# Matrix products of a tile of ones in TensorE's three waits for the routing of a mixture of experts

## The chip, the cores and the metric

The kernel runs on one core of a Trainium2 chip. The metric is the device time of one execution in microseconds (us). TensorE (PE in the profile) has two clock levels in the rows, 1.2 and 2.4 GHz: the column PEclk gives the granted share, 0.50 for the lower and 1.00 for the upper.

## The reference, cut to what matters

One layer of an encoder on 512 tokens of width 1024: token mixing (retention and differential attention behind one input projection), then a mixture of 16 gated experts with two chosen for each token, then an embedding added under a gate. What surrounds the change is the choice of experts:

```python
lg = (t @ w_rg) + b_rg                      # 4 groups, the best one is taken
le = ((t @ w_re) + b_re).reshape(-1, 4, 4)  # 4 experts in each, the best two are taken
top_v, top_i = lax.top_k(le_sel, 2)
combine = one_hot(g_idx)[:, :, None] * w_in_group[:, None, :]
...
hid = silu(t @ w_gate[e]) * (t @ w_up[e]) * combine[:, e]
out = out + hid @ w_down[e]
```

All is float32. An expert has 4 MB of w_gate and w_up together and 2 MB of w_down; all 16 experts are loaded.

## The kernel before, in words

The kernel is written engine by engine, and the engines meet only through semaphores. Each engine works off its own list in the order in which it is written.

**Ahead of the routing.** TensorE makes the output projection with three products for each part (lines 1348 to 1350), transposes the new x (line 1519) and multiplies it by the router's weights (line 1532, 20 columns). VectorE adds the projection to x (line 1227, semaphore `x1_add`, which ends at 16) and norms it (line 1233). TensorE then transposes the input p of the last stage, eight transposes of 128x128 (line 1558).

**The routing**, on VectorE in `route()` (lines 971 to 1080), with TensorE used three times:

- VectorE finds the chosen experts and sums the membership (line 1014, `member_ready`). TensorE makes ranks from it in two products, line 1562 (ones times prefix, 80 columns) and line 1563 (64 columns), into `b_rank`.
- VectorE makes slots and one-hot tables from the ranks (lines 1022 to 1046, `slot_oh_ready`). TensorE sums with them the row numbers of every block, line 1567: two groups of eight products of 128x28, the first for the rows to be read, the second for the rows to be written.
- After the first group VectorE writes `src_row` (line 1054) and GpSimd issues the gathers of the first two blocks of rows (line 679). After the second it writes `dst_row` (line 1059) and the codes of the blocks (lines 1060 to 1070, `table_ready`).

**The experts.** The tokens are sorted by expert into blocks of 64 places, here 20 blocks. For a block TensorE transposes the gathered rows (line 1608, in `rows_transpose`), multiplies by w_gate and w_up (line 1622, in `gate_up`, 16 products of float32 that stand as 32 instructions), transposes the hidden part (line 1634) and multiplies by w_down (line 1648, in `down`). The order is: rows of block 0, `gate_up(0)`, rows of block 1, and then for each b: `hidden_transpose(b-1)`, `gate_up(b)`, rows of b+1, `down(b-1)`.

**The weights.** A ring of three places holds them. SyncE (SP, its queue SPq) issues the loads in a fixed order (line 586 for w_gate and w_up in halves, line 589 for w_down), and the load of expert e+3 waits until TensorE has used expert e: `gu_half_done`, `gu_done`, `dn_done`. The w_down of expert 2 waits for `table_ready` and for the gathered rows (lines 612 to 615). Experts 0 and 1 and the w_gate and w_up of expert 2 are under way before the routing ends.

**The clock.** At its start the kernel multiplies a tile of ones by itself 24 times before any data is there (line 1356), and 12 times while it waits for the first weights (line 1478). A float32 product stands as two matrix instructions and two weight loads in the trace.

Of the kernel before, what the change touches and what calls it, by code (L numbers as in the profile page):

```python
# [36 lines left out]
P = 128  # L37
SEQ, D = 512, 1024
NT = SEQ // P
# [31 lines left out]
OUT_UNITS = D // UC  # L71
# [136 lines left out]
def trunk(nc, x, p, norm_mix, w_in, lam_q1, lam_k1, lam_q2, lam_k2, diff_subln, w_out, norm_ffn,  # L208
# [3 lines left out]
    with ctx:  # L212
# [3 lines left out]
        def at(name, kb, shape, dt=F32):  # L216

            return nc.alloc_sbuf_tensor_at(name, shape, dt, offset=base + int(kb * K))
# [38 lines left out]
        ones = at("ones", 98.75, [P, P])  # L257
# [140 lines left out]
        b_proj = [bank[0], bank[1], bank[7]]  # L398
# [8 lines left out]
        def sem(name):  # L407
            return ctx.enter_context(nc.semaphore(name))
# [58 lines left out]
        x1_add = sem("x1_added")  # L467
# [874 lines left out]
        def _(pe):  # L1342
            T = nc.tensor
# [212 lines left out]
            for c in range(D_PLE // P):  # L1556
                for t in range(NT):
                    last = T.transpose(b_score[c][:, t * P:(t + 1) * P], p_sb[:, t, c * P:(c + 1) * P], ident)
                last.then_inc(p_T, 1)

            pe.wait_ge(member_ready, 1)
            T.matmul(b_rank[:, 0:80], ones[:], prefix[:].rearrange("p i e -> p (i e)"), start=True, stop=False)
            T.matmul(b_rank[:, 0:64], tri, member[:, 1:].rearrange("p i e -> p (i e)"), start=False, stop=True).then_inc(rank_done, 1)
            for w in range(2):
                pe.wait_ge(slot_oh_ready, 1 + w)
                for n in range(2 * NT):
                    last = T.matmul(b_rows[w],  # L1567
                                    slot_oh[:, n, :], blk_rows[:, w, n, :],
                                    start=(n == 0), stop=(n == 2 * NT - 1))
                last.then_inc(rows_done, 1)  # L1570

            pe.wait_ge(pT_ready, 2)
            pe.wait_ge(table_ready, 1)
# [166 lines left out]
```

## Time and profile before

| | |
|---|---|
| median of 3 runs | 637.39 us (636.6 to 638.26) |
| the profiled execution's own time | 636.99 us |
| its span, first to last instruction | 635.1 us |
| TensorE busy | 589.0 us, 93% of the span |
| mean granted TensorE clock | 0.967 |
| DMA packets | 151.52 MB, mean 239 GB/s |

Times in the rows count from the span's first instruction. The profiled execution's own time lies 1.9 us above its span. "issue" in the chain is time in which an engine waited for nothing that the profile shows. A number such as x32 behind a group counts instructions.

### The profile page before, as it was taken

The numbers are of one execution on the slowest core, as the hardware profiler recorded it, in microseconds if no ns is written. First come the engines' busy times: TensorE is split into PE (matmuls) and PEld (weight loads), VectorE is DVE, ScalarE is ACT, GpSimd is POOL, SyncE is SP. The second block draws the span as 40 slices with busy tenths as digits, with TensorE's granted clock in tenths as the row PEclk, the third lists the DMA queues.
The fourth block names the chain that finished last, engine by engine and source line by source line (L and its number), as shares of the span: only waits on it lengthen the run. The fifth ranks groups of instructions, "written<-read, shape, count | busy, mean of one in ns | idle before, by whom it ended". The sixth has DMA issues, their size and how long they took to land.

```text
span 635.1 us, 9546 instructions
## 1 busy us (share of the span) xinstructions
PE 589.0 (93%) x3496; PEld 386.2 (61%) x3497; DVE 209.7 (33%) x460; ACT 199.0 (31%) x435; POOL 51.1 (8%) x89
## 2 busy tenths in 40 slices
PE   9999999999999999975769999999999987998994
PEld 9988777878988999974223333333333332335883
DVE  4521365456344342265101111011011010164753
ACT  5622254545443543240100010010010010073774
POOL 0000000000000000001101211211212211110000
PEclk9999999999999999995789999999999999998998
DMA  9852214213220249737994799999999999934001
GB/s 310 221 203 99 71 63 133 67 32 101 68 67 1 67 160 419 316 136 296 362 418 183 296 418 425 422 418 422 419 422 422 420 421 421 393 120 179 34 33 66
DMA packets 47232, 151.52 MB, mean 239 GB/s; under 512 B 7896, under 2 KB 27232, under 8 KB 34656
## 3 DMA queue, kind: packets, MB, share of 16 engines
q1 hardware_dynamic: 43520, 139.77, 56.3%
q0 software_dynamic: 3392, 11.02, 4.4%
q8 instruction: 22, 0.36, 0.2%
q10 hardware_dynamic: 288, 0.29, 0.2%
q14 instruction: 10, 0.08, 0.0%
HBM read 141.62 MB, written 9.45 MB: 238 GB/s over the span
## 4 chain that ended last, share of the span: by engine, by line
PE 83%; DMA 5%; DVE 4%; issue 3%; SPq 2%; ACT 2%; DVEq 0%; POOL 0%; ACTq 0%; POOLq 0%
PE bank L1622 19%; PE bank L1348 13%; PE bank L1349 12%; PE bank L1350 12%; PE bank L1648 10%; DMA ring_dn<-in_w_down 5%; PE bank L1430 2%; PE bank L1681 2%; SPq L586 2%; PE bank L1608 2%; PE bank L1403 2%; PE bank L1356 1%; PE bank L1634 1%; PE bank L1567 1%; PE bank L1444 1%
## 5 line engine op out<-in xcount | busy, mean ns | idle before, releaser
L1622 PE MATMUL bank<-ring_gu,rowsT 128*64 128x512 f32 (+1 forms) x800 | 144.7, 602 | 6.4 <-DMA ring_gu<-in_w_up 2.8
L1622 PEld LDWEIGHTS bank<-ring_gu,rowsT 128*64 128x64 f32 (+1 forms) x800 | 43.9, 128 | 92.4 <-issue 88.1
L1648 PE MATMUL bank<-ring_dn,hidT 128*64 128x512 f32 (+1 forms) x400 | 74.7, 607 | 9.8 <-issue 5.2
L891 ACT ACTIVATE silu_g<-bank 128x256 f32<-128x256 f32 x20 | 7.7, 384 | 221.8 <-PE bank L1622 221.8
L1087 DVE TENSOR_TENSOR w_lo<-w_raw,w_hi 128x2048 fp32r<-128x2048 f32 x17 | 39.0, 2293 | 76.7 <-ACT w_hi L752 64.9
L1246 DVE TENSOR_TENSOR hid<-silu_g,bank 128x256 f32<-128x256 f32 x20 | 8.4, 421 | 147.9 <-ACT silu_g L891 147.9
L1348 PE MATMUL bank<-w_hi,hT_hi 128*128 128x256 f32 x192 | 55.5, 289 | 0.8 <-issue 0.6
L1349 PE MATMUL bank<-w_lo,hT_hi 128*128 128x256 f32 x192 | 54.3, 283 | 0.0
L1350 PE MATMUL bank<-w_hi,hT_lo 128*128 128x256 f32 x192 | 54.3, 283 | 0.0
L1348 PE MATMUL bank<-hT_hi,w_hi 128*128 128x512 f32 x128 | 50.9, 397 | 0.1
L1648 PEld LDWEIGHTS bank<-ring_dn,hidT 128*64 128x64 f32 (+1 forms) x400 | 21.0, 128 | 48.4 <-issue 42.3
L1349 PE MATMUL bank<-hT_lo,w_hi 128*128 128x512 f32 x128 | 50.0, 390 | 0.0
L1350 PE MATMUL bank<-hT_hi,w_lo 128*128 128x512 f32 x128 | 49.9, 390 | 0.0
L1260 DVE COPY y_blk<-bank 128x512 f32<-128x512 f32 x20 | 13.8, 692 | 80.7 <-PE bank L1648 80.7
L1348 PEld LDWEIGHTS bank<-w_hi,hT_hi 128*128 128x128 f32 x192 | 36.7, 191 | 2.6 <-issue 2.5
L1349 PEld LDWEIGHTS bank<-w_lo,hT_hi 128*128 128x128 f32 x192 | 36.8, 192 | 0.0
L1350 PEld LDWEIGHTS bank<-w_hi,hT_lo 128*128 128x128 f32 x192 | 36.8, 191 | 0.0
L752 ACT ACTIVATE w_hi<-w_raw 128x2048 fp32r<-128x2048 f32 x17 | 32.4, 1906 | 0.0
L1348 PEld LDWEIGHTS bank<-hT_hi,w_hi 128*128 128x128 f32 x128 | 24.0, 188 | 8.3 <-issue 3.6
L1348 PE MATMUL bank<-ple_hi,x2T_hi 128*128 128x512 f32 x64 | 25.8, 404 | 2.5 <-issue 2.5
L1350 PEld LDWEIGHTS bank<-hT_hi,w_lo 128*128 128x128 f32 x128 | 24.0, 188 | 5.1
L1349 PEld LDWEIGHTS bank<-hT_lo,w_hi 128*128 128x128 f32 x128 | 24.0, 188 | 4.7
(217 smaller groups left out, 892.7 us busy)
## 6 DMA issues: line engine op xcount, KB each, us to landing
ring_gu<-in_w_gate SPq DMA_DIRECT2D x32, 1024.0 KB, 12.3
ring_gu<-in_w_up SPq DMA_DIRECT2D x32, 1024.0 KB, 15.3
ring_dn<-in_w_down SPq DMA_DIRECT2D x16, 2048.0 KB, 21.5
w_raw<-in_w_in SPq DMA_DIRECT2D x13, 1024.0 KB, 5.0
w_raw<-in_w_out SPq DMA_DIRECT2D x4, 1024.0 KB, 4.9
ple_gate_raw<-in_w_ple_gate SPq DMA_DIRECT2D x1, 4096.0 KB, 28.9
yg<-y_rows SPq DMA_DIRECT2D x8, 512.0 KB, 7.2
xr<-in_x SPq DMA_DIRECT2D x4, 512.0 KB, 8.8
```

The source lines that it names most:

```text
L586: sp.dma_start(ring_gu[slot][:, n, ks, :], src[:, half]).then_inc(s_gu[slot][half], 16)
L752: nc.scalar.activation(w_hi[u % 2][:], w_raw[u % 2][:], ACT.Copy).then_inc(hi_done, 1)
L1087: V.tensor_tensor(w_lo[u % 2][:], w_raw[u % 2][:], w_hi[u % 2][:].bitcast(F32), ALU.subtract).then_inc(lo_done, 1)
L1260: V.tensor_copy(y_blk[buf][:], b_dn[:]).then_inc(y_ready, 1)
L1348: T.matmul(o, w_of(w[0], k), m_of(m[0], k), start=(k == 0), stop=False)
L1349: T.matmul(o, w_of(w[0], k), m_of(m[1], k), start=False, stop=False)
L1350: last = T.matmul(o, w_of(w[1], k), m_of(m[0], k), start=False, stop=(k == KD - 1))
L1403: last = T.matmul(b_score[2 * (i % 2) + c][:, 0:L], dqT[64 * c:64 * c + 64, h, i * P:(i + 1) * P], dkT[64 * c:64 * c + 64, h, 0:L], start= ...
L1430: last = T.matmul(b_o[:, i * P:(i + 1) * P], probsT[n % 2][:, o:o + P], v[:, j, h * P:(h + 1) * P], start=(j == 0), stop=(j == i))
L1608: last = T.transpose(b_xT[:, j * P:(j + 1) * P], rows[buf][:, j::4], ident)
L1622: last = T.matmul(b_gu[q * BLK + t:q * BLK + t + n, :], rowsT[:, k % 4, k // 4, t:t + n], ring_gu[s][:, :, k, q * UC:(q + 1) * UC], start= ...
L1648: last = T.matmul(b_dn[q * BLK + t:q * BLK + t + n, :], hidT[:, kf % 2, kf // 2, t:t + n], ring_dn[s][:, kf, q * (D // 2):(q + 1) * (D // 2)],
```

## The change

TensorE gets a helper that multiplies the 128x128 tile of ones by itself n times into the first 128 columns of the bank `b_proj[2]`, whose last sum has been taken when `x1_add` is 16. It is called with 10, 14 and 10: before the wait for `member_ready`, after the rank products, and after the row-number products. Nothing is removed, and no other engine's list changes.

```diff
                 last.then_inc(p_T, 1)
 
+            def kept_warm(n):
+                for _ in range(n):
+                    T.matmul(b_proj[2][:, 0:P], ones[:], ones[:], start=True, stop=True)
+
+            pe.wait_ge(x1_add, NT * OUT_UNITS)
+            kept_warm(10)
             pe.wait_ge(member_ready, 1)
             T.matmul(b_rank[:, 0:80], ones[:], prefix[:].rearrange("p i e -> p (i e)"), start=True, stop=False)
             T.matmul(b_rank[:, 0:64], tri, member[:, 1:].rearrange("p i e -> p (i e)"), start=False, stop=True).then_inc(rank_done, 1)
+            kept_warm(14)
             for w in range(2):
                 pe.wait_ge(slot_oh_ready, 1 + w)
                 for n in range(2 * NT):
...
                 last.then_inc(rows_done, 1)
+
+            kept_warm(10)
 
             pe.wait_ge(pT_ready, 2)
             pe.wait_ge(table_ready, 1)
```

## Rows read from the trace of the kernel before

**Rows 1.** The page's clock line, in 40 equal slices of the span.
```profile
PEclk9999999999999999995789999999999999998998
```

**Rows 2.** Stretches: busy us of each engine, PEclk, DMA share, GB/s.
```profile
core 0: us, PE busy (x) PEld busy (x) DVE busy (x) ACT busy (x) POOL busy (x), PEclk, DMA share, GB/s
340.00:350.00 10.00, 10.00 (x52) 3.56 (x52) 1.45 (x3) 0.98 (x2) 1.05 (x2) 1.00 0.43 171
360.00:545.00 185.00, 178.46 (x1016) 61.47 (x1014) 22.68 (x47) 14.71 (x30) 35.80 (x61) 1.00 1.01 421
```

**Rows 3.** TensorE's timeline near the end of the experts: start, us, group, idle before.
```profile
539.62 3.65 PE L1648 MATMUL bank<-ring_dn,hidT 128*64 128x512 f32 x16 [1.84 <-DMA ring_dn<-in_w_down]
```

**Rows 4.** SyncE's timeline: two weight loads that follow one another.
```profile
336.05 0.38 SPq L589 DMA_DIRECT2D ring_dn<-in_w_down  x1
353.02 0.34 SPq L586 DMA_DIRECT2D ring_gu<-in_w_gate  x1
```

**Rows 5.** The chain that ended last, from the ranks to the first product with w_down: start, us.
```profile
286.82 0.72 PE bank L1562 x2
287.54 0.41 PE bank L1563 x2
...
291.82 7.04 PE bank L1567 x32
...
301.75 0.99 issue
302.74 1.14 PE bank L1608 x4
...
304.73 9.75 PE bank L1622 x32
...
317.55 7.09 PE bank L1622 x32
324.64 0.68 PE bank L1608 x4
325.32 5.16 issue
330.47 5.38 PE bank L1648 x16
```

**Rows 6.** Short stretches around changes of clock or pace, columns as in rows 2.
```profile
5.50:6.00 0.50, 0.50 (x4) 0.50 (x4) 0.00 (x0) 0.47 (x3) 0.00 (x0) 1.00 1.03 285
6.50:7.00 0.50, 0.50 (x7) 0.50 (x6) 0.00 (x0) 0.00 (x0) 0.00 (x0) 1.00 1.07 360
...
282.50:282.75 0.25, 0.25 (x3) 0.06 (x1) 0.22 (x2) 0.25 (x1) 0.00 (x0) 1.00 0.00 0
282.75:283.00 0.25, 0.04 (x1) 0.00 (x0) 0.21 (x2) 0.25 (x2) 0.00 (x0) 0.57 0.62 246
...
310.00:310.25 0.25, 0.25 (x4) 0.14 (x2) 0.00 (x0) 0.00 (x0) 0.00 (x0) 0.82 0.89 328
```

**Rows 7.** Ones (chain), and the work ahead of the first wait (timeline).
```profile
0.98 8.15 PE bank L1356 x48
10.01 2.68 PE bank L1478 x24
...
280.81 0.97 PEld L1532 LDWEIGHTS bank<-w_r,x1T 128*128 128x128 f32 x8 [1.13 <-ACT x1T L851]
281.72 1.07 PE L1558 MATMUL bank<-small,p_sb 128*128 128x128 f32 x8
```

**Rows 8.** The first gather (timeline), gathers' time to landing, a stretch.
```profile
296.67 1.03 POOL L679 DMA_INDIRECT rows<-h_rows,src_row  x1 [294.69 <-DVE src_row L1054]
...
rows<-h_rows,src_now POOLq DMA_INDIRECT x20, 7.1
rows<-h_rows,src_row POOLq DMA_INDIRECT x2, 3.5
...
296.00:298.00 2.00, 2.00 (x11) 2.00 (x11) 0.62 (x1) 0.00 (x0) 1.03 (x2) 0.50 0.08 33
```

## The prediction

> **What bounds the kernel now.** I read the stretches first, then the chain, then the clock. From 360 to 545 us the DMA engines are full (share 1.01, 421 GB/s) and the clock is 1.00; near its end TensorE waits for w_down [rows 2, 3]. So the experts' second half is bound by bytes. But from 340 to 350 us the DMA share is 0.43 with TensorE busy all the time [rows 2]: SyncE has issued a load at 336.05 and issues the next at 353.02, when TensorE is halfway through `gate_up(3)` [rows 4]. The stream of weights that fills the rest of the kernel starts when TensorE lets it. What TensorE gains before 353 us brings the stream forward, and with it the end; what it gains between 353 us and the last weights is hidden behind them.
>
> The chain of that stretch is TensorE and VectorE in turn [rows 5]: ranks at 286.82, row numbers from 291.82 to 298.86, table ready at 301.75, transposes at 302.74, `gate_up(0)` for 9.75 us, `gate_up(1)` for 7.09 us. The two products are the same work, so 2.66 us of the first are the clock. It is the only low place of length in the clock line, slices 19 to 21, about 286 to 333 us [rows 1]. In short stretches one sees the edges: 1.00 until 282.75, then 0.57 in the quarter in which the last transpose ends, and up again in the quarter from 310.00 [rows 6]. Thus the ranks, the row numbers, the rows' transposes and over half of `gate_up(0)` run at 1.2 GHz.
>
> **The price of the ones.** 24 of their matrix instructions at the upper level take 2.68 us, 0.112 us each; the 48 at the start take 8.15 us [rows 7]. With twice 0.112 us at the lower level, n of 48 low gives 0.223n + 0.112(48-n) = 8.15, so n = 25 or 5.6 us. The stretches show the pace change from 4 to 7 starts in half a microsecond in that place [rows 6] (the PEclk column reads 1.00 there from the start; the pace is the witness). So a run of these products alone did raise the clock here, after 5 to 6 us.
>
> **Part 1, ten products before the ranks** (20 instructions: 2.2 us at 2.4 GHz, 4.5 us at 1.2). They start behind the transposes at 282.8; the ranks' wait ends at 286.82, 4.0 us of cover. The clock falls at 282.8, before the first of them has run, so they can't prevent that fall; I take them as starting low. Low throughout they end at 287.3 and cost 0.5 us; if the clock comes back on the way they cost nothing. I take a cost of 0.2, ends 0 and 0.5.
>
> **Part 2, the ranks.** 0.72 + 0.41 = 1.13 us at 1.2 GHz [rows 5]; at 2.4 at best half, a gain of 0 to 0.5. I take 0.4. VectorE's work behind them, 287.95 to 291.82 (3.87 us), moves with them.
>
> **Part 3, fourteen products after the ranks** (28 instructions: 3.1 us high, 6.2 low). The cover is those 3.87 us. High they cost nothing; low they make the row numbers 2.4 us late. I take 0.
>
> **Part 4, the row numbers.** 32 instructions in 7.04 us, 0.22 each, at 1.2 GHz. The nearest rows at 2.4 GHz are the router's loads of 128 columns before 20 moving columns: eight from 280.81 until the next line's work at about 281.7, 0.11 each [rows 7]. So at best the 7.04 us become 3.5. I don't take all of it: in the trace 7 us of these narrow products left the clock low, and it fell after about two microseconds of 20-column products and transposes. I expect the first group high and the second low or the reverse: a gain of 1.75, ends 0 and 3.5.
>
> A rule speaks against this part. The Trainium skill (TensorE: Matmul & The Clock Gate, section "LDWEIGHTS") gives a weight load as its columns over 1.2, with no regard to the clock. By it the row numbers, which are loads above all, would gain nothing, and the sum below would be 1.75 less. The rows disagree, 0.22 us each low against 0.11 high, and I go by the rows.
>
> **Part 5, ten products after the row numbers.** The cover is the way to the transposes, 298.86 to 302.74, 3.9 us: 2.2 us high are hidden, 4.5 low are 0.6 late. I take 0. If this work were not there, nothing else would hold the clock in that wait.
>
> **Beside it: the gathers.** The first is issued at 296.67, just as the weights' transfer has drained (share 0.08 in 296 to 298), and lands in 3.5 us; with full queues a gather takes 7.1 [rows 8]. With the first group ready some 2.2 us sooner it is issued at 294.5 into a full queue and lands between 298.0 and 301.6. The table asks for the transposes at 302.74 - 1.95 = 300.8, so it costs 0 to 0.8 us; I take 0. SyncE's load of w_down behind it isn't used before block 2.
>
> **Part 6, transposes and `gate_up(0)`.** 1.14 against 0.68 us is a gain of 0.46, and 9.75 against 7.09 one of 2.66 [rows 5], if the clock is up at their start.
>
> **Sum.** -0.2 + 0.4 + 1.75 + 0.46 + 2.66 = 5.1 us sooner at the end of `gate_up(0)`. What follows up to 353 us is on the chain and moves with it: the gap of 5.16 us before the first `down` too, behind which that product takes 5.38 us instead of 3.65 [rows 3, 5]. Whether the clock falls in that gap again I can't tell; I assume that it does, and 1.7 us more are to be had if not. The loads of 301 to 333 us are not in the way, since the DMA share of 0.43 leaves room to come forward by more than this. Against the profiled time, 636.99 - 5.1 = 631.9; the median of the runs stands 0.4 above it, so I predict **632.3 us**.
>
> **Rivals.**
>
> *The clock is lost again before `gate_up(0)`* (0.12). The last things before it are transposes and a wait. For it: it fell at 282.8 right behind the p transposes. Then only 0.4 - 0.2 + 1.75 = 1.95 us are gained, 635.4, and `gate_up(0)` still takes 9.75. The Trainium skill (same page, "PE-mode transpose") says that a transpose doesn't count as work for the clock; the fall at 282.8 behind eight of them agrees.
>
> *Slower: the ones run low throughout* (0.06). If neither the first ten nor the fourteen raise the clock, the ranks start 0.5 late, the fourteen take 6.2 us against a cover of 3.87 and make the row numbers 2.4 later, and the last ten another 0.6: 3.5 us, 640.9. The point is whether the clock is up before about 289, while the fourteen run. Against it: alone at the start the ones did raise it.
>
> *Hidden after all* (0.05). If the weights' stream rather than TensorE sets the start of the bound part, 637.4. For it: the share of 1.01; against it: 0.43 in 340 to 350.
>
> *The loads of weights don't follow the clock* (0.04). 5.1 - 1.75 = 3.3 us, 634.1. This is the page's rule of part 4.
>
> *The change does nothing* (0.03). The products run in the waits, but the clock stays as it was where it matters, and no wait is lengthened: 637.4.
>
> *The forecast* has 0.70, from 3.5 to 7.1 us (part 1 at 0, part 2 at 0.5, part 4 at 3.5) with up to 1.7 for `down(0)`.
>
> **Numbers.** Low end: 637.4 - 7.1 - 0.7 (part of the 1.7) = 629.6. High end: up to the case in which the clock is lost, 635.4 and half a microsecond of scatter, 635.9. A measurement of this kernel can tell about 0.3%, 1.9 us, so faster is below 635.5: the forecast 0.70, the rule's rival 0.04 and half of the lost clock 0.06, together 0.80. Same: the other half 0.06, 0.05 and 0.03, together 0.14. Slower 0.06.
>
> **What would show it.** Part 1: 20 instructions of ones from 282.8, PEclk 0.50 at first, 1.00 before 288. Part 4: the row numbers in 3.5 to 5.5 us instead of 7.04. Part 6: `gate_up(0)` near 7.1 us, its start near 300 to 302. The load of 353.02 issued about 5 us sooner, the same share of 1.01 from there on. I am wrong if the clock reads 0.50 when `gate_up(0)` starts, if the row numbers wait for ones, or if the load at 353 comes sooner and the end doesn't.

## The result, and the profile after

The changed kernel takes 629.38 us (median of 4 runs, 626.58 to 631.16) against 637.83 us before in the same comparison: 8.4 us less, ratio 0.9852 with an interval of 0.9824 to 0.988. The forecast was 632.3 us in a range from 629.6; the direction was right, the gain forecast too small, and the median lies 0.2 us under the range. The profiled execution of the changed kernel took 630.97 us, 1.6 above its median.

The page's head, its clock line and its row for the queue that carries instructions:

```profile
span 629.1 us, 9682 instructions
...
PEclk9999999999999999998899999999999999988998
...
q8 instruction: 23, 0.38, 0.3%
```

The 136 instructions more are the 34 products of ones, two matrix instructions and two weight loads each. The clock line has two places of 8 where [rows 1] have 5, 7, 8. One more low place has come up late, at slice 36.

The chain that ended last, in the same stretch as [rows 5] (start, us, what; L1563 is now the ones, L1568 and L1569 the ranks, L1574 the row numbers, L1617 the rows' transposes, L1631 `gate_up`, L1643 the hidden transposes, L1657 `down`):

```profile
286.52 0.45 PE bank L1568 x2
...
287.18 4.81 PE bank L1563 x28
291.98 1.72 PE bank L1574 x16
...
294.92 3.54 DMA rows<-h_rows,src_row
298.46 0.90 issue
299.36 0.76 PE bank L1617 x4
...
300.97 8.80 PE bank L1631 x32
...
312.71 7.09 PE bank L1631 x32
...
320.48 0.72 issue
321.20 3.65 PE bank L1657 x16
324.86 0.91 issue
...
326.27 1.46 issue
327.72 8.78 PE bank L1631 x32
```

Against [rows 5]: the transposes come at 299.36 instead of 302.74, and `gate_up(0)` takes 8.80 instead of 9.75 us. The product of `gate_up(0)` ends at 309.77 instead of 314.48, 4.7 us earlier. Then comes what the forecast had not: the gap of 5.16 us before the first `down` is 0.72 us, and there is one of 0.91 behind it. With the gap gone `down(0)` takes 3.65 instead of 5.38 us, but `gate_up(2)` falls into a low clock and takes 8.78 us instead of 7.09, so that these two cancel. By 336.5, the end of `gate_up(2)`, TensorE is 8.0 us ahead.

Two stretches show where the clock is low now (columns as in [rows 2]), and SyncE's load that answers to the second of [rows 4]:

```profile
287.50:291.00 3.50, 3.50 (x19) 3.50 (x18) 3.26 (x11) 0.00 (x0) 0.00 (x0) 0.51 1.01 426
301.00:305.00 4.00, 4.00 (x12) 1.31 (x14) 0.00 (x0) 1.24 (x2) 0.97 (x1) 0.57 0.93 336
```
```profile
344.99 0.34 SPq L586 DMA_DIRECT2D ring_gu<-in_w_gate  x1
```

The load is issued 8.03 us earlier. From there the DMA engines are full, and what TensorE has gained arrives at the end, less 2 us: the last `down` fell into a low clock in this execution (5.35 us where it took 3.65 before), which is the late place in the clock line.

```profile
549.88 5.35 PE L1657 MATMUL bank<-ring_dn,hidT 128*64 128x512 f32 x16 [0.84 <-DVE hidT L1251]
```

So the 8 us at 345 us have two parts: about 4.7 up to the end of `gate_up(0)` (0.3 of them because VectorE is 0.3 earlier from long before the change), and 3.3 behind it. The second part stands where neither a product of ones nor a change of clock was expected. Two theories can explain it. **Code**: 34 products more move all of TensorE's later instructions, code comes in transfers of 16 KB, and a transfer that TensorE had to wait for while the DMA engines were full is no longer in that place. **Clock**: all of it follows from the clock, through the times at which transfers start.

### The profile page after: what moved, and what is told of

It reads as the page before. It is cut to its first block, busy times and chain, and to the rows that moved or that the text cites. A ratio compares the mean times of both kernels' runs of the same rounds, so it can differ in the third digit from the quotient of the medians.

```text
span 629.1 us, 9682 instructions
## 1 busy us (share of the span) xinstructions
PE 595.5 (95%) x3564; PEld 391.3 (62%) x3565; DVE 209.7 (33%) x460; ACT 199.3 (32%) x435; POOL 51.3 (8%) x89
## 4 chain that ended last, share of the span: by engine, by line
PE 82%; DMA 7%; DVE 3%; issue 3%; ACT 2%; SPq 2%; DVEq 0%; POOLq 0%; ACTq 0%
PE bank L1631 19%; PE bank L1348 13%; PE bank L1349 13%; PE bank L1350 13%; PE bank L1657 10%; DMA ring_dn<-in_w_down 5%; PE bank L1430 2%; PE bank L1690 2%; SPq L586 2%; PE bank L1617 2%; PE bank L1403 2%; PE bank L1643 1%; PE bank L1444 1%; DMA gmix<-in_norm_mix 1%; PE bank L1563 1%
## 5 line engine op out<-in xcount | busy, mean ns | idle before, releaser
L1631 PE MATMUL bank<-ring_gu,rowsT 128*64 128x512 f32 (+1 forms) x800 | 145.5, 604 | 5.1 <-issue 2.9
L1631 PEld LDWEIGHTS bank<-ring_gu,rowsT 128*64 128x64 f32 (+1 forms) x800 | 44.1, 128 | 91.4 <-issue 87.8
L1657 PE MATMUL bank<-ring_dn,hidT 128*64 128x512 f32 (+1 forms) x400 | 76.4, 616 | 5.5 <-DMA ring_dn<-in_w_down 4.0
L1657 PEld LDWEIGHTS bank<-ring_dn,hidT 128*64 128x64 f32 (+1 forms) x400 | 21.5, 129 | 45.4 <-issue 39.1
```

The costliest lines, as they stand in the source:

```text
L1631: last = T.matmul(b_gu[q * BLK + t:q * BLK + t + n, :], rowsT[:, k % 4, k // 4, t:t + n], ring_gu[s][:, :, k, q * UC:(q + 1) * UC], start= ...
L1657: last = T.matmul(b_dn[q * BLK + t:q * BLK + t + n, :], hidT[:, kf % 2, kf // 2, t:t + n], ring_dn[s][:, kf, q * (D // 2):(q + 1) * (D // 2)],
```

## The experiments

**The same code without the work.** The tile of ones is replaced by products of one column by one column in the same places:

```diff
+            def tiny(n):
+                for _ in range(n):
+                    T.matmul(b_proj[2][0:1, 0:1], ones[:, 0:1], ones[:, 0:1], start=True, stop=True)
...
-            kept_warm(10)
+            tiny(10)
...
-            kept_warm(14)
+            tiny(14)
...
-            kept_warm(10)
+            tiny(10)
```

> All 34 products of ones become products of one column by one column in the same places: the same number of TensorE instructions and the same code size as in the changed kernel, and next to no matrix work. Code theory (part of the gain is that TensorE's code lies elsewhere, so that the 5.16 us gap before the first down product is gone whatever the clock does): the gap is about 0.7 us as in the changed kernel, the clock is low from 283 to about 310 as before, gate_up(0) takes near 9.7 us, and the time is 2 to 4 us under the kernel before, 634 to 636. Clock theory (all comes from the clock): the gap stays at 5 us and the time is that of the kernel before, 637 to 638.

Measured: 633.77 us (5 runs), before 638.2 (14 runs), ratio 0.9945, 0.9926 to 0.9963. Code alone, with hardly any work, makes the kernel faster: 4.4 us by the medians, 3.5 by the ratio. Its chain:

```profile
301.76 0.99 issue
302.76 1.14 PE bank L1621 x4
...
304.75 9.62 PE bank L1635 x32
...
325.84 1.03 issue
326.88 5.34 PE bank L1661 x16
```

Up to `gate_up(0)` it is the kernel before, to within 0.15 us: the clock is low for it. The gap ahead of `down` (L1661) is 1.03 us, with one of 0.70 ahead of the transposes. The clock theory expected 637 to 638 and a gap of 5 us; it falls as the only cause.

**The work with the old place of the code.** Thirty one-column products are added to the changed kernel, 256 TensorE instructions in all, matrix products and weight loads together. If an instruction takes 64 bytes, they are the 16 KB of one transfer:

```diff
             kept_warm(10)
+            tiny(15)
...
             kept_warm(10)
+            tiny(15)
```

> The changed kernel with 30 one-column products more (15 behind the first ten products of ones, 15 behind the last ten), so that 256 matrix instructions are added in all where the change adds 136. One transfer of code carries 16 KB; if an instruction takes 64 bytes, all code behind lies at the same place within its 16 KB as in the kernel before. Code theory: the gap of about 5 us before the first down product comes back, and the time is 2 to 4 us above the changed kernel, 631 to 634. Clock theory: the time of the changed kernel, 628 to 630, with at most 0.5 us for the longer waits.

Measured: 636.23 us (10 runs), ratio 0.9968, 0.9945 to 0.9992. The gap is back, 5.82 us, although the row numbers take 3.9 us, nearly all at the upper clock:

```profile
291.76 3.90 PE bank L1579 x32
...
321.80 5.82 issue
327.62 6.20 PE bank L1663 x16
```

It took 2 us more than expected. The gap lets the clock fall again: `down` takes 6.20 us instead of 3.65. And the third wait was overfilled: ones and one-column products end at 300.28, so that the transposes come at 300.68, 1.3 us later than in the changed kernel. Whether the two explain all of the 2 us isn't shown.

**The fourth corner**: 64 one-column products and no ones, 256 instructions too.

```diff
-            kept_warm(10)
+            tiny(20)
...
-            kept_warm(14)
+            tiny(24)
...
-            kept_warm(10)
+            tiny(20)
```

> The kernel before with 64 one-column products in the three waits (20, 24, 20) and no product of ones: 256 matrix instructions added and nearly no matrix work. Code theory: with 16 KB of code added, the code behind lies in its transfers of 16 KB as in the kernel before; the gap of about 5 us before the first down product is back and the time is that of the kernel before, 637 to 638.5. Rival, any addition of code takes the gap away or the one-column products help by themselves: 633 to 635, as with 34 of them.

Measured: 637.28 us (10 runs), before 638.51 (19 runs), ratio 0.9981, 0.9963 to 0.9999. The gap is there, and the time is that of the kernel before but for at most a few tenths of a per cent:

```profile
324.92 5.64 issue
330.56 6.43 PE bank L1661 x16
```

The four corners don't simply add up. Without the gap the ones take the time from 633.8 to 629.4 us; with it only from 637.3 to 636.2, and there the intervals of the two ratios overlap.

**Other amounts of code.** Eight and twenty one-column products behind the first ten of ones, and 42 of them without ones:

```diff
             kept_warm(10)
+            tiny(8)
```


> The changed kernel with 8 one-column products behind the first ten of ones: 32 instructions or 2 KB more code, otherwise the same. Code theory: the gaps ahead of the first gate_up, down and hidden transposes move by 2 KB of code; if none comes to lie on the wrong side of a transfer, 628 to 631 as the changed kernel, else up to 5 us more. Clock theory: 628 to 631.

```diff
             kept_warm(10)
+            tiny(20)
```


> The changed kernel with 20 one-column products behind the first ten of ones: 80 instructions or 5 KB more code, between the changed kernel (no large gap) and the one with 120 instructions more (a gap of 5.8 us). Code theory: the sum of the gaps before block 3 lies between theirs and names where the large gap begins; 629 to 636. Clock theory: 628 to 631.

```diff
-            kept_warm(10)
+            tiny(18)
...
-            kept_warm(14)
+            tiny(14)
...
-            kept_warm(10)
+            tiny(10)
```


> The kernel before with 42 one-column products (18, 14, 10) and no product of ones: 168 instructions, the code size of the changed kernel with 8 one-column products. Code theory: the large gap before the first down product is away as with 34 of them, 632 to 635. Rival, that the 34 one-column products won by chance of the clock: 637 to 638.

Measured: 627.15 us (4 runs), 635.83 (10 runs) and 634.25 (4 runs, ratio 0.9929, 0.9906 to 0.9953). The first two differ by twelve cheap products, 48 instructions, and by 8.7 us; the third, 168 instructions without ones, stays near the 633.8 us of 136. With twenty the gap has come back in another place, between `down(0)` and the hidden transposes (L1648), and the low clock behind it is in `gate_up(2)`:

```profile
321.33 4.08 PE bank L1662 x16
325.41 6.01 issue
331.42 0.69 PE bank L1648 x2
332.11 1.25 issue
333.37 9.93 PE bank L1636 x32
```

One count sorts all of them. The queue q8 carries instructions; in the stretch from 300 to 350 us, the first pass through the experts' code, it has this row in the changed kernel and the next in the kernel before:

```profile
q8 instruction: 4, 0.07, 0.5%
```
```profile
q8 instruction: 5, 0.08, 0.6%
```

| kernel | instructions added | ones | transfers of q8, 300 to 350 | longest gap, us | load that starts the bound part, us | median, us |
|---|---|---|---|---|---|---|
| before | 0 | no | 5 | 5.16 | 353.02 | 637.8 to 638.5 |
| 34 one-column | 136 | no | 4 | 1.45 | 348.78 | 633.8 |
| 42 one-column | 168 | no | 4 | 1.59 | 349.03 | 634.3 |
| 64 one-column | 256 | no | 5 | 5.64 | 353.01 | 637.3 |
| changed | 136 | 34 | 4 | 1.46 | 344.99 | 629.4 |
| changed, 8 more | 168 | 34 | 4 | 1.66 | 344.76 | 627.2 |
| changed, 20 more | 216 | 34 | 5 | 6.01 | 351.78 | 635.8 |
| changed, 30 more | 256 | 34 | 5 | 5.82 | 350.05 | 636.2 |

Four transfers and no long gap, or five and one of 5 to 6 us, whatever the ones do. The other profiles of this document with the weights' loads left as they were have four, and no gap above 1.6 us. A transfer less in this stretch isn't a transfer less in all: the changed kernel and those with 136 or 168 one-column instructions have one at 295 to 297 us, during the routing, where the kernel before has none. How a 16 KB block comes to be late for just one place, and why 216 instructions move the gap behind `down(0)`, isn't shown.

**Is the gap a transfer under load?** The kernel before, with SyncE held back until the first `down` is done:

```diff
+            sp.wait_ge(dn_done, 1)
             reload_gu(RING, 0)
```

> The kernel before with one wait more on SyncE: the loads of expert 3 and later are not issued before the first down product is done, so that the DMA engines are empty when TensorE comes to the 5.16 us gap. If the gap is a transfer of TensorE's code that is slow because it shares the DMA engines with 4 MB of weights, it shrinks to 1 to 3 us here; if it is a cost of TensorE's own, it stays at 5. The time isn't the question: the weights come later, and I expect 637 to 650.

Measured in one execution each: 640.22 us beside 638.16. The weights come later, as expected. With TensorE's code as before and five transfers in the same stretch, the gap is gone and `down` follows the transposes at once. Its chain, and then a stretch ahead of the gap in this kernel and in the kernel before (DMA share 0.12 against 1.02):

```profile
324.44 0.68 PE bank L1609 x4
325.12 3.58 PE bank L1649 x16
```
```profile
318.00:324.00 6.00, 6.00 (x30) 1.93 (x26) 0.00 (x0) 0.00 (x0) 0.00 (x0) 1.00 0.12 40
```
```profile
318.00:324.00 6.00, 6.00 (x30) 2.08 (x28) 0.00 (x0) 0.00 (x0) 0.00 (x0) 1.00 1.02 422
```

The row of q8 for 318 to 333 us, first in the kernel before, then in this one:

```profile
q8 instruction: 3, 0.05, 1.3%
```
```profile
q8 instruction: 4, 0.07, 1.6%
```

By the trace the three start at 320.55, 326.50 and 332.40 us, 5.9 us apart, and TensorE stands still from 325.32 to 330.47. The four start at 318.08, 321.13, 324.20 and 327.26, 3.1 us apart. A transfer's own packet lasts about 1 us in both; what grows under load is the distance from one to the next.

So the 5 us need both: a transfer of code in that place, and DMA engines full of weights.

**Which ones do what.** With the code size of the changed kernel, only the last ten are of ones, or only the first 24:

```diff
-            kept_warm(10)
+            tiny(10)
...
-            kept_warm(14)
+            tiny(14)
...
             kept_warm(10)
```


> Only the last ten products are of ones, the first 24 are of one column: the code size of the changed kernel. If the clock for the row numbers is what the first 24 bring, the row numbers take 7.0 us here instead of 3.5 and the time is about 3 us above the changed kernel, 632 to 633, with the clock up in part of gate_up(0) because of the last ten. If the last ten products alone bring nothing for gate_up(0), it takes 9.7 us and the time is that of the kernel with one-column products everywhere.

```diff
             kept_warm(10)
...
             kept_warm(14)
...
-            kept_warm(10)
+            tiny(10)
```


> The first 24 products are of ones, the last ten of one column: the code size of the changed kernel. If the last ten hold the clock for gate_up(0), it takes about 9.7 us here instead of 8.8 or 7.1, and the time is 1 to 2.5 us above the changed kernel, 630 to 632. If the clock holds without them, the time is that of the changed kernel, 628 to 630. The row numbers take 3.5 us in either case.

Measured: 630.36 us (ratio 0.9895, 0.987 to 0.9921) and 630.39 us (0.9887, 0.987 to 0.9904), 4 runs each: 1 us above the changed kernel and 3.4 us under the one with none. TensorE's timelines, first with the last ten only, then with the first 24 only:

```profile
291.85 7.03 PE L1578 MATMUL bank<-blk_rows,slot_oh 128*128 128x28 f32 x32 [3.11 <-DVE slot_oh L1045]
298.70 3.98 PE L1563 MATMUL bank<-ones 128*128 128x128 f32 x20
...
304.39 7.09 PE L1635 MATMUL bank<-ring_gu,rowsT 128*64 128x512 f32 x32 [0.87 <-ACT rowsT L886]
```
```profile
291.41 3.75 PE L1578 MATMUL bank<-blk_rows,slot_oh 128*128 128x28 f32 x32 [0.70 <-DVE slot_oh L1045]
295.10 0.64 PE L1567 MATMUL bank<-ones 128*1 128x1 f32 x20
299.07 1.12 PE L1621 MATMUL bank<-small,rows 128*128 128x128 f32 x4 [3.33 <-DMA rows<-h_rows,src_row]
301.06 9.72 PE L1635 MATMUL bank<-ring_gu,rowsT 128*64 128x512 f32 x32 [0.87 <-ACT rowsT L886]
```

In the place behind each filling it divides cleanly. The first 24 buy the row numbers, 7.03 to 3.75 us; the last ten buy `gate_up(0)`, 9.72 to 7.09. In time it doesn't: either half alone is worth 3.4 us, both together 4.4. With the last ten only, `gate_up(1)` falls into the low clock instead and takes 8.78 us, and the time is 1.6 us below the 632 to 633 that were expected.

**Closing the last gaps.** In the changed kernel's profile the clock is low from 301 us, at the start of `gate_up(0)`, behind the wait for the gathered rows and the one for their evacuation. Both are filled:

```diff
-            kept_warm(10)
+            kept_warm(16)
...
             rows_transpose(0, 1)
+            kept_warm(3)
```

> The changed kernel with 16 instead of 10 products of ones in the third wait and 3 more between the first transposes of rows and gate_up(0), where TensorE waits 0.87 us. If the clock fell at the start of gate_up(0) because of the two waits ahead of it, it now stays up: gate_up(0) in 7.1 us instead of 8.8, and the time is 1 to 2 us under the changed kernel, 627 to 629. If the fall comes all the same, the time is that of the changed kernel or 0.5 us over it. The code grows by 36 instructions, 2.3 KB, as in the kernel with 8 one-column products.

Measured: 627.08 us (4 runs), ratio 0.9815, 0.9778 to 0.9852. It was timed again beside the changed kernel:

> The kernel with 16 products of ones in the third wait and 3 more ahead of gate_up(0), once more. If the clock at the start of gate_up(0) is what it gains over the changed kernel, it is 1 to 2 us under it here too, 626 to 629; if its 2.3 KB of code more were the cause instead, it should equal the kernel with 8 one-column products, 627, and both its gaps and the clock in the profile tell which.

> The changed kernel once more, timed beside the next one on the same chip. Both theories: 628 to 631.

Measured: 626.21 us (5 runs, ratio 0.9821, 0.98 to 0.9841) against 629.31 us for the changed kernel (6 runs, 0.9869, 0.9847 to 0.9892) on the same chip. It is the fastest version here, 12.1 us or 1.8% under the kernel before. In both profiles `gate_up(0)` takes 7.11 us; the first of them:

```profile
302.51 7.11 PE bank L1635 x32
```

This was the expectation, but it doesn't account for the gain. In the profile of the changed kernel that was taken beside it, `gate_up(0)` takes 7.11 us too, without the added ones. Pieces of the two chains, first the changed kernel's, then that of the one with both waits filled:

```profile
300.42 7.11 PE bank L1631 x32
...
318.16 0.71 issue
...
322.53 1.51 issue
...
324.54 1.36 issue
325.90 8.78 PE bank L1631 x32
```
```profile
311.86 8.78 PE bank L1635 x32
...
325.34 0.47 issue
```

Each has one `gate_up` at the low clock, `gate_up(2)` in the first and `gate_up(1)` in the second. What differs are the waits around `down(0)` that stand as "issue", 3.6 us against 0.5, which leave the second 1.8 us ahead when the load that starts the bound part is issued (343.17 and 341.38). Nearly all the rest between these two executions is the last `down`, 5.35 against 3.65 us. So the 3.1 us between the medians are shown as a gain, but not as one of the clock at `gate_up(0)`, and how much of them the 2.3 KB of code more make isn't settled: the changed kernel with 2 KB more code and no more ones reached 627.15 us, though with only 4 runs spread over 4.4 us.

## Why the prediction was wrong

**The step that failed** is in the sentence behind the sum: "What follows up to 353 us is on the chain and moves with it: the gap of 5.16 us before the first `down` too". I had the gap in front of me as "issue", an engine that waits for nothing that the profile shows, and took an unexplained wait for a constant. By the experiments it was a wait for TensorE's own code, and 34 products are 136 instructions of code. In the changed kernel the waits from the transposes of block 1 to `gate_up(2)`, 5.16 and 1.16 us before, are 0.72, 0.91 and 1.46. The rule was at hand. The Trainium skill (Advanced Engine Details and Errata, section "ISA Cache") says that instructions are cached in lines of 16 KB, each of 256 instructions. The runs agree: a transfer of q8 carries 16 KB, 256 instructions added bring the gap back, and 136 and 168 take it away; 216 bring one back too, in another place. The forecast held no price for code at all, for or against; the same change with 80 instructions more takes 635.8 us, 2.7 us under the kernel before.

What the code was worth with no ones: 638.2 to 633.8 us. What the ones were worth at equal code: 633.8 to 629.4 us, 4.4 us, where the sum had 5.1. The missing term is thus about as large as the one I had. They aren't independent: the forecast kept the gap, and with the gap in place (30 one-column products more) the ones reached only 636.2 us, 2.0 under the kernel before, part of the shortfall being the overfilled third wait. That the forecast of 632.3 us came within 3 us of the result is in part luck.

The sentence behind that step, on `down(0)`, was wrong too. I assumed that the clock falls in the gap again, and put 0.7 of the 1.7 us into the low end of the range. With the gap gone the product took 3.65 us, the whole 1.7; `gate_up(2)`, which the forecast didn't price, lost as much.

**Part 1** said that the clock falls at 282.8, before the first product of ones. In the changed kernel's profile it didn't: the first ten took 2.40 us at the upper level, and the fall came at 287.5, among the fourteen. In its second profile the ten took 3.52 us, partly low, and in the kernel with the first 24 only 3.87 us. Both occur, so the place of the fall isn't tied to the transposes' end as one trace had made it look. The ranks were on time in all three.

**Part 2**, 0.4 forecast: 1.13 to 0.66 us, 0.5. Right.

**Part 3**, no cost forecast: the fourteen took 4.81 us, part of them low, against a cover of 3.87, and the row numbers began 0.9 us late. For this execution the choice of 0 was wrong by 0.9. In the second profile the fourteen ran at the upper level, 3.34 us, and cost nothing, so the term varies from run to run.

**Part 4**, 1.75 forecast, ends 0 and 3.5: 7.04 to 3.5 us, the whole of it. Clock and loads go together: 32 pairs of load and product take 7.03 us at 0.50 and 3.65 to 3.75 at 1.00 in the timelines. The Trainium skill's figure for a weight load, the same at either clock (TensorE: Matmul & The Clock Gate, section "LDWEIGHTS"), doesn't fit these rows; the measurement decides, and that rival is out.

**Part 5 and the gathers**, no cost: table and gathered rows were ready within 0.1 us of each other. The first gather landed in 3.54 us, no slower than before [rows 8], at 298.46; the transposes followed at 299.36. Right.

**Part 6**, 0.46 and 2.66 forecast: 0.38 and 0.95 in the profiled execution, since the clock fell at 301 and was back before 305. In the second profile of the changed kernel, and in the one with the last ten only, `gate_up(0)` had the whole 2.66. The forecast took the best case of a term that varies from run to run.

Up to the end of `gate_up(0)` the sum was 5.1 and the profile has 4.4 without the head start of 0.3: the errors of parts 3, 4 and 6 nearly cancel, which is luck. **The bound part** was right: the load at 353.02 came 8.03 us sooner, the DMA share stayed at 1.01, and the end followed. **The rivals**: the clock was lost at the start of `gate_up(0)` in one profile of the changed kernel, for about 1.7 us of cost, and not in the other; slower, hidden and nothing didn't occur.

## What to carry to other kernels

Where an engine waits for nothing that the profile shows while the DMA engines are full, count the instruction queue's transfers in that stretch: it may be waiting for its own code. Then a change that adds or removes instructions upstream is two changes, and a control with the same number of instructions and no work (here products of one column) tells them apart. Filling TensorE's waits with products does pay where the work behind the wait is on the path, but look at the products further on as well: in several of these profiles a later `gate_up` took 8.78 us, partly at a low clock, instead. And the filling is safe only if it is shorter than the wait at the lower clock too: fourteen products in a wait of 3.87 us cost nothing in one profile and 0.9 us in another.

## What the runs showed of the hardware that I had not expected

- Instructions arrive in transfers of 16 KB, and with weights filling the DMA engines (share 1.02) one such transfer in the wrong place is a wait of 5.2 to 6.0 us on TensorE; with the engines nearly empty (0.12) there was no such wait. One block follows another after 5.9 us under load and after 3.1 without it.
- The amount of code ahead moved the time by up to 8.7 us, more than the products of ones did. Two kernels that differ by 48 cheap instructions took 627.2 and 635.8 us.
- The same kernel's clock falls in different places from run to run: in two profiles of the changed kernel the first ten products of ones took 2.40 and 3.52 us, and `gate_up(0)` 8.80 and 7.11.
